# A hybrid layer and two conditioned layers on one core: inputs of rotation issued on SyncE, part of the preparations moved beside the first projection, modulations' sums by rounded products

## The chip, the core and the metric

One core of a Trainium2 chip runs the kernel. The time is the device time of one execution in microseconds (us). The engines are TensorE (PE; PEld is its loading of the stationary operand), VectorE (DVE), ScalarE (ACT), GpSimd (POOL) and SyncE (SP). An "ACTq" or "SPq" row is an instruction of an engine's queue that issues a transfer.

## What is computed

512 tokens of width 1024, all float32. First one hybrid layer:

```python
proj = rmsnorm(x) @ w_in                       # 8 chunks of columns, then the merge gates
ys = (gated_deltanet(...), spatial_gating(u, v, z, ...), rwkv7_time_mix(...), native_sparse_attention(...))
mixed = sum(sigmoid(merge_i) * (ys[i] @ w_branch[i]))
x = rmsnorm(x + mixed @ w_out)
```

Spatial gating is `u * (tril(w_s) @ layernorm(v) + b_s) * silu(z)` in chunks of 128 tokens and four groups of 64 columns. The sparse attention needs a small MLP over blocks of 32 keys (compression) and three tables of distance by slope, masked. Then two layers, each with

```python
mod = silu(c) @ ada_w[l] + ada_b[l]            # 1024 x 6144, one row: shifts, scales, gates
x = x + gate_m * mixer(norm(x) * (1 + scale_m) + shift_m)      # differential and dilated attention, rotated q, k
x = x + gate_f * relu(h @ w_mlp_up)**2 @ w_mlp_down
```

## The kernel before

The kernel is one program of stages. A stage is a block with one list of instructions per engine; between blocks all engines meet (`end_stage` resets the counts that the waits use). Order inside a stage is written out by hand with semaphores (`Signal`); there is no planner. The residual stream `xT` lies in SBUF, features on partitions.

Dense products are made to float32 accuracy from rounded parts: ScalarE copies an operand to float32r (the "hi" part), VectorE subtracts it from the original (the "lo" part), and TensorE adds three rounded products hi x hi, hi x lo, lo x hi in a bank. In the projections (`first_projection` L925, `queries_keys`, `values`) a weight chunk of up to 512 columns is split in four pieces ahead of its use, one piece per tile; in `split_products` (L2304: merge, gates, output) and `mlp` (L3033) the splitting goes on piece by piece, four pieces (two tiles in the MLP) ahead of TensorE. Weights come through a ring of three slots of 2 MB that SyncE fills (`Weights.feed` L251); it waits in its queue for the release of a slot.

The stages that matter here, in order:

- `first_projection`: 33 tiles (t = 0 to 32) in 8 banks; TensorE needs a bank emptied 8 tiles earlier. Tiles 16 to 19 are u and v of gating (gelu on ScalarE), 20 to 23 two gates (silu), 24 to 27 "ab", 28 to 32 keys. ScalarE and VectorE each go through the tiles in order: split a piece of the next chunk, convolve or shift a row, empty a bank. At the end SyncE moves two halves of the keys, once tile 28 is emptied.
- `preparations` (L1282): its inputs are issued at its start, nine on SyncE (L1557 to L1565), six on ScalarE's queue (L1364 to L1368). TensorE: transposes w_s (L1429), transposes the positions (L1432), gate products of RWKV (L1423, L1424), the hidden layer of the compression (L1440, 64 products on halves of the array), gating's products (L1449), compressed keys and values (L1455, L1457), eight transpositions of y (L1462). VectorE has one list: blocks (L1479), decay sums, mean and variance of gating (L1487 to L1497), tables (L1502 to L1506), gate additions (L1512), copy of w_s (L1521), normalisation (L1523 to L1527), g, y (L1540, L1552, L1553), and POOL masks the tables.
- `sparse_attention` with `attention`, then `operands` (L1658), whose end is transpositions into features; the last are those of the sparse attention's y (L1788), copied by ScalarE (L1850). `recurrences` follow.
- `merge` (L2483): 96 pieces, beside which a guest, `Modulation(self, 0)` (L425), forms the first layer's modulations; the MLP of layer 0 holds `Modulation(self, 1)`. The guest loads 1 MB halves of ada_w (issued on ScalarE), VectorE multiplies and adds eight rows of 512 columns (one operation per piece, two per tile in the MLP), and TensorE sums each of the twelve results over partitions (`turn`, L466): four float32 products with one column of ones.
- the output product (`add_products`) with `Turns` (L511) beside it: 13 small inputs (positions, gains) issued by ScalarE ahead of all its work (`beside.load(act)`), tables of sine and cosine on VectorE from its fifth piece on. `RowTail` squares and copies each finished row. `values` of layer 0 has `Reach` beside it, with four inputs, issued the same way.

Of the kernel before, what the change touches and what calls it, by code (L numbers as in the profile page):

```python
# [424 lines left out]
class Modulation:  # L425


    HALVES = 24
    OPS = 4

    def __init__(self, kernel, l):
        self.kernel, self.l = kernel, l
        self.w, self.acc = kernel.take(2, 4, 512), kernel.take(2, 512)
        self.source = kernel.a["ada_w_2"][l]
        self.loads = self.ops = self.turns = 0
# [10 lines left out]
    def multiply(self, dve):  # L446
# [6 lines left out]
        if n % 8 == 0:  # L453
            if c >= 2:
                dve.wait_ge(*k.mod_turned.at(c - 1))
# [10 lines left out]
    def turn(self, pe):  # L466
        k, c = self.kernel, self.turns
        pe.wait_ge(*k.ada_used.at(2 * c + 2))
        for j in range(4):
            ins = pe.matmul(k.bank[7][:, 4 * c + j:4 * c + j + 1], self.acc[:, c % 2, j * P:(j + 1) * P], k.ones[:, 0:1],  # L470
                            start=True, stop=True)
        ins.then_inc(*k.mod_turned.one())
        self.turns += 1

    def finish(self, dve):
        k, l = self.kernel, self.l
        assert self.ops == 4 * self.HALVES
        dve.wait_ge(*k.mod_turned.at(self.HALVES // 2))
        b = PAR["ada_b_2"] + 48 * l
        mod = k.mods[:, l, :]  # L480
        dve.tensor_tensor(mod, k.bank[7][:, 0:48], k.par[:, b:b + 48], ALU.add).then_inc(*k.mod_row.one())
# [7 lines left out]
class RowTail:  # L489
# [7 lines left out]
    def scalar(self, act, k):  # L497
# [3 lines left out]
        if self.by_class is not None:  # L501
# [9 lines left out]
class Turns:  # L511
# [3 lines left out]
    def __init__(self, kernel):  # L515
        R = E // 4 // 2
        self.kernel = kernel
        self.cos, self.sin = kernel.take(NT, R), kernel.take(NT, R)
        self.gains = [kernel.take(2, 2, E) for _ in range(2)]
        self.pos, self.ang, self.n = kernel.take(NT), kernel.take(NT, R), kernel.take(NT, R)  # L520
        kernel.turns = kernel.take(2, 2, 2, NT * 4 * R)
        kernel.row_gain = kernel.take(2, 2, 2)
# [182 lines left out]
class Kernel:  # L705
    def __init__(self, nc, arrays, out):
# [13 lines left out]
        self.arena = sb("arena", [P, ARENA])  # L720

# [25 lines left out]
        self.stored = Signal(nc, "stored")  # L747
        self.moved = Signal(nc, "near_values_moved")
# [22 lines left out]
        self.mod_turned = Signal(nc, "mod_turned")  # L771
# [153 lines left out]
    def first_projection(self):  # L925
        nc = self.nc
# [17 lines left out]
        self.nsa_cmpT = self.take(T)  # L944
        acc = self.take(2, T)
        assert self.top <= ARENA - 2 * SLOT
        self.top -= 2 * T
# [28 lines left out]
        with nc.Block() as block:  # L976
# [28 lines left out]
            def _(act):  # L1005
                for k in range(ND):
                    norm.first_part(act, h[0][:, k, :], k).then_inc(*h_first.one())
                for t, (name, kind, i, lo, n) in enumerate(tiles):
                    if self.w.next_hi < self.w.pieces_until(("p1", name), place[t] + 1):
                        self.w.split_hi(act)  # L1010
                    if t - 2 in convolved:
# [3 lines left out]
                           .then_inc(*self.mixed_act.step(("silu", c)))  # L1015
                    if kind == "features":
                        continue
# [21 lines left out]
            def _(dve):  # L1039
# [21 lines left out]
                def shift(c):  # L1061
# [7 lines left out]
                       .then_inc(*self.mixed_dve.step(("shift", c)))  # L1069
                for t, (name, kind, i, lo, n) in enumerate(tiles):  # L1070
                    if self.w.next_lo < self.w.pieces_until(("p1", name), place[t] + 1):
# [18 lines left out]
            def _(pool):  # L1090
                pool.memset(qkvT[:, :, 0:3], 0.0).then_inc(*self.pool_order.one())
                pool.memset(rwT[:, :, 0:1], 0.0).then_inc(*self.pool_order.one())

            @block.sync
            def _(sp):
                self.w.feed(sp)
                keys = [t for t, tile in enumerate(tiles) if tile[:2] == ("keys", "features")][0]
# [184 lines left out]
    def preparations(self):  # L1282


        nc, a = self.nc, self.a
# [4 lines left out]
        self.y_nsa = self.ysT[:, 0:2, :].rearrange("p k t -> p (k t)").rearrange("p (i c) -> p i c", i=NT)  # L1290
# [20 lines left out]
        self.kcT = self.take(NC)  # L1311
        self.vc = self.take(E)
        self.sel = self.take(H, T)
        self.win = self.take(H, 3 * P)
        self.cmp = self.take(NT, H, NC)
        self.seen = self.take(NT, NC)
        self.gsum = self.take(H)
        keep = self.top
        sel, win, cmp, seen = self.sel, self.win, self.cmp, self.seen
        SLOPES = [2.0 ** (-8.0 * (h + 1) / H) for h in range(H)]  # L1320
        dist = self.scratch[:]
# [5 lines left out]
        def in_h(n, *dims):  # L1327
# [4 lines left out]
        w1, w2, pos_rows, posT = in_h(32, E), in_h(2, E), in_h(2, E), in_h(2, 32)  # L1332
        blocks, hidden = in_h(32, NC), in_h(2, NC)

        gain, bias = self.take(MIX), self.take(MIX)
        w_rows, wT = self.take(H, P), self.take(H, P)
        y, sq = self.take(NT, MIX), self.take(NT, MIX)
        mean, rstd = self.take(NT, H), self.take(NT, H)
        groups = lambda x: x.rearrange("p i (g c) -> p i g c", g=H)
        over = lambda x: x.unsqueeze(3).broadcast_to([P, NT, H, E])  # L1340
        u, v, z = (self.sg[:, :, j * MIX:(j + 1) * MIX] for j in range(3))

        dtb, alog = self.take(H), self.take(H)
        low, small = self.take(NT, H), self.take(NT, H)
        w0a0, up = self.take(2 * MIX), self.take(MIX)
        rwT = self.rwT

        landed = [self.params_landed, self.x_landed, self.moved]
        compress, gating, mixers = landed
        mm, act_done, dve_done, pool_done = self.mm_done, self.act_ready, self.dve_ready, self.pool_ready  # L1350
        mm.order_of(["wT", "pos", ("wa", 0), "hidden0", "hidden1", ("wa", 1), "mixed0", "mixed1", "kc", "vc",
                     ("y", 0), ("y", 1)])
        act_done.order_of(["tanh", "softplus", "alog", "root", "hidden0", "hidden1", ("wa", 0), ("wa", 1), "beta", "cond",
                           ("y", 0), ("y", 1)])
# [1891 lines left out]
```

## Time and profile before

| | us |
|---|---|
| runs: median of 3 (lowest, highest) | 2890.76 (2886.28, 2893.64) |
| the profiled execution | 2882.78 |
| its span, first to last instruction | 2881.0 |
| TensorE busy | 2600.3 (90%) |
| VectorE busy | 1601.1 (56%) |
| ScalarE busy | 1047.2 (36%) |

The time of the profiled execution is its span and a little around it. Busy time is the union of an engine's instructions. A row of a timeline gives the start in us from the span's start, the duration in us (of a merged group: from its first start to its last end), engine, line, operation, output<-inputs, shape and count; in brackets the idle time of the engine before it and what ended it. A matmul of float32 operands that are not rounded stands as two instructions.

### The profile page before, as it was taken

To read this page: it belongs to the slowest core of one execution; us is meant where nothing else is said; L and a number is where in the kernel's file an instruction comes from. 1 tells how busy PE (TensorE), PEld (TensorE's weight loads), DVE (VectorE), ACT (ScalarE), POOL (GpSimd) and SP (SyncE) were. 2 spreads that over 40 slices of the span, in tenths; PEclk is the share of its full clock that TensorE was granted. 3 is DMA by queue.
4 is the path that set the end of the run, shared out by engine and by line. 5 is a ranking of instruction groups with operands and counts; after the bars stand their busy time and mean duration, and the time that the engine had idled before them with its cause. 6 is when DMAs were issued, how large, how long until landed. Compare 5 with 4: busy or idle time off the path is not lost. (4 is left out here: it accounts for less than half of the span.)

```text
span 2881.0 us, 37978 instructions
## 1 busy us (share of the span) xinstructions
PE 2600.3 (90%) x15005; PEld 2078.3 (72%) x15005; DVE 1601.1 (56%) x3039; ACT 1047.2 (36%) x2148; POOL 22.1 (1%) x68
## 2 busy tenths in 40 slices
PE   6986688799889897889989999899979999899999
PEld 5875577688668656767768888687557777688887
DVE  5616756766566586353366765553865333454444
ACT  3225432333355364352332222353644432322221
POOL 0002000000000000000000000000000000000000
PEclk8996888899989998999999999999989999899999
DMA  4220020466412200203335553221002223222220
GB/s 147 78 55 5 10 58 3 132 206 191 152 59 88 93 1 15 84 25 95 112 129 178 184 181 117 88 84 63 30 1 71 53 72 106 88 88 88 102 103 30
DMA packets 212218, 249.56 MB, mean 87 GB/s; under 512 B 13295, under 2 KB 125898, under 8 KB 212042
## 3 DMA queue, kind: packets, MB, share of 16 engines
q1 hardware_dynamic: 178608, 194.22, 20.9%
q10 hardware_dynamic: 33434, 52.91, 5.6%
q8 instruction: 120, 1.97, 0.3%
q14 instruction: 56, 0.46, 0.1%
HBM read 243.70 MB, written 2.10 MB: 85 GB/s over the span
## 5 line engine op out<-in xcount | busy, mean ns | idle before, releaser
L2378 ACT ACTIVATE weights_hi<-weight_ring 128x512 fp32r<-128x512 f32 (+1 forms) x240 | 143.9, 602 | 427.3 <-PE bank L2432 392.6
L2400 DVE TENSOR_TENSOR weights_lo<-weight_ring,weights_hi 128x512 fp32r<-128x512 f32 (+1 forms) x240 | 156.2, 654 | 230.7 <-ACT weights_hi L2378 230.5
L3061 ACT ACTIVATE weights_hi<-weight_ring 128x1024 fp32r<-128x1024 f32 x128 | 135.2, 1057 | 262.9 <-PE bank L3157 261.6
L2432 PE MATMUL bank<-h_hi,weights_hi 128*128 128x512 f32 x512 | 209.8, 410 | 15.8 <-DVE h_lo L2400 8.9
L3157 PE MATMUL bank<-h_hi,weights_hi 128*128 128x512 f32 x512 | 204.4, 399 | 13.0 <-DVE h_lo L422 12.2
L2585 PE MATMUL bank<-chunk_hi,h_hi 128*128 128x512 f32 x448 | 185.2, 413 | 21.2 <-DVE h_lo L422 17.4
L2432 PE MATMUL bank<-h_lo,weights_hi 128*128 128x512 f32 x512 | 204.0, 398 | 0.0
L3157 PE MATMUL bank<-h_lo,weights_hi 128*128 128x512 f32 x512 | 203.6, 398 | 0.0
L2432 PE MATMUL bank<-h_hi,weights_lo 128*128 128x512 f32 x512 | 202.0, 395 | 0.0
L3157 PE MATMUL bank<-h_hi,weights_lo 128*128 128x512 f32 x512 | 201.8, 394 | 0.0
L3157 PE MATMUL bank<-hidden_hi,weights_hi 128*128 128x512 f32 x512 | 199.8, 390 | 0.0
L3157 PE MATMUL bank<-hidden_hi,weights_lo 128*128 128x512 f32 x512 | 199.3, 389 | 0.0
L3157 PE MATMUL bank<-hidden_lo,weights_hi 128*128 128x512 f32 x512 | 199.2, 389 | 0.0
L2585 PE MATMUL bank<-weight_ring_lo,h_hi 128*128 128x512 f32 x448 | 178.9, 399 | 0.0
L2585 PE MATMUL bank<-chunk_hi,h_lo 128*128 128x512 f32 x448 | 177.6, 396 | 0.0
L2432 PE MATMUL bank<-hidden_hi,weights_hi 128*128 128x512 f32 x384 | 152.7, 398 | 20.5 <-DVE hidden_lo L2400 20.5
L3099 DVE TENSOR_TENSOR weights_lo<-weight_ring,weights_hi 128x1024 fp32r<-128x1024 f32 x128 | 156.4, 1222 | 20.5 <-ACT weights_hi L3061 20.4
L460 DVE SCALAR_TENSOR_TENSOR arena<-arena,cond 128x512 f32<-128x512 f32 x168 | 126.1, 751 | 60.0 <-PE bank L2432 57.9
L2432 PE MATMUL bank<-hidden_lo,weights_hi 128*128 128x512 f32 x384 | 151.7, 395 | 0.0
L2432 PE MATMUL bank<-hidden_hi,weights_lo 128*128 128x512 f32 x384 | 151.5, 395 | 0.0
L1197 PE MATMUL bank<-arena 128*128 128x128 f32 (+1 forms) x984 | 135.4, 282 | 6.6 <-ACT arena L1268 6.4
L3129 DVE SCALAR_TENSOR_TENSOR xT<-bank,modulations,xT 128x512 f32<-128x512 f32 x64 | 48.0, 751 | 162.6 <-PE bank L3157 162.6
(487 smaller groups left out, 5377.8 us busy)
## 6 DMA issues: line engine op xcount, KB each, us to landing
arena<-in_ada_w ACTq DMA_DIRECT2D x48, 1024.0 KB, 5.3
weight_ring<-in_w_in SPq DMA_DIRECT2D x21, 2048.0 KB, 7.6
weight_ring<-in_w_in SPq DMA_DIRECT2D x65, 512.0 KB, 5.3
weight_ring<-in_w_mlp_up SPq DMA_DIRECT2D x16, 2048.0 KB, 8.9
weight_ring<-in_w_mlp_down SPq DMA_DIRECT2D x16, 2048.0 KB, 8.0
weight_ring<-in_w_out SPq DMA_DIRECT2D x6, 2048.0 KB, 7.9
weight_ring<-in_w_in SPq DMA_DIRECT2D x10, 1024.0 KB, 7.6
weight_ring<-in_w_branch_a SPq DMA_DIRECT2D x16, 512.0 KB, 6.4
```

The costliest lines, as they stand in the source:

```text
L460: ins = dve.scalar_tensor_tensor(acc, self.w[:, half, j, :], by, acc, ALU.mult, ALU.add)
L1197: ins = pe.matmul(self.bank[O_BANK + g % 2][:, lo:hi], turned[0:k, n % 2, b * P:(b + 1) * P], v, start=b == 0, stop=b == len(u["values"]) - 1)
L2378: act.activation(hi, src, ACT.Copy).then_inc(*hi_done.one())
L2400: dve.tensor_tensor(lo, src, hi.bitcast(F32), ALU.subtract).then_inc(*lo_done.one())
L2432: ins = pe.matmul(out, ws[a_][:, n % PIECES, k - k0, :], tile["x"][b_][:, k, :], start=k + a_ + b_ == 0, stop=last[n] and k == k1 - 1 and ...
L2585: ins = pe.matmul(self.bank[n % 3][:, 0:width], h[a_][:, k, i * P:(i + 1) * P], w[b_][:, k, :], start=k + a_ + b_ == 0, stop=k == ND - 1 a ...
L3061: act.activation(ws[0][:, t % 2], src[t // 4][:, :, c % 4 * P:c % 4 * P + P], ACT.Copy)\
L3099: dve.tensor_tensor(ws[1][:, t % 2], src[t // 4][:, :, c % 4 * P:c % 4 * P + P], ws[0][:, t % 2].bitcast(F32), ALU.subtract).then_inc(*lo_ ...
L3129: dve.scalar_tensor_tensor(self.xT[:, c, :], self.bank[t % NB][:], gate(c), self.xT[:, c, :], ALU.mult, ALU.add).then_inc(*out.one())
L3157: ins = pe.matmul(self.bank[t % NB][:], ws[a_][:, t % 2, k, :], x[b_][:, k, :], start=k + a_ + b_ == 0, stop=k == ND - 1 and a_ == 1)
```

## The change

1. `Turns` and `Reach` issue their inputs on SyncE, ahead of the weights of that stage. `Turns`' lasting tables come first in memory.
2. All inputs of `preparations` are issued by SyncE in `first_projection`, into two ring slots that are free by then. Gating's normalisation and the sparse attention's tables run on VectorE between tiles 22 and 29, their masks on POOL; tanh, cond and the root of the variance on ScalarE.
3. In `preparations`, blocks are formed on 128 partitions; both pairs of gate products have banks of their own and stand first; the transpositions of gating's y move to the end of `operands`.
4. `Modulation`: the accumulated row is split in hi and lo, and two rounded products with a 128x128 of ones give the column sums in all partitions; VectorE takes the diagonals. Nine operations per eight pieces in the merge.
5. `RowTail` squares before it copies.

```diff
 class Modulation:
-    def turn(self, pe):
-        k, c = self.kernel, self.turns
-        pe.wait_ge(*k.ada_used.at(2 * c + 2))
-        for j in range(4):
-            ins = pe.matmul(k.bank[7][:, 4 * c + j:4 * c + j + 1], self.acc[:, c % 2, j * P:(j + 1) * P], k.ones[:, 0:1],
-                            start=True, stop=True)
...
+    def scalar(self, act, n):
+        while 2 <= self.loads < self.HALVES and self.half_done(self.loads - 2) <= n - 2:
+            self.load(act)
+        c = self.due(n, 0)
+        if c is not None:
+            act.wait_ge(*k.ada_used.at(2 * c + 2))
+            if c:
+                act.wait_ge(*k.mod_summed.at(c))
+            act.activation(self.hi, self.acc[:, c % 2, :], ACT.Copy).then_inc(*k.mod_first.one())
+    def tensor(self, pe, n):
+        c = self.due(n, 2)
+        if c is not None:
+            pe.wait_ge(*k.mod_second.at(c + 1))
...
+            pe.matmul(k.bank[7], self.ones, self.hi, start=True, stop=False)
+            pe.matmul(k.bank[7], self.ones, self.lo[c % 2], start=False, stop=True)\
+              .then_inc(*k.mod_summed.one())
+    def vector(self, dve, n):
+        for _ in range(self.steps(n)):
+            if self.ops < self.HALVES * self.OPS:
+                self.multiply(dve)
+        c = self.due(n, 1)
+        if c is not None:
+            dve.wait_ge(*k.mod_first.at(c + 1))
+            dve.tensor_tensor(self.lo[c % 2], acc, self.hi.bitcast(F32), ALU.subtract).then_inc(*k.mod_second.one())
+        c = self.due(n, 3)
+        if c is not None:
+            dve.wait_ge(*k.mod_summed.at(c + 1))
+            dve.tensor_tensor(own, k.bank[7].rearrange("p (j q) -> p j q", j=4),
+                              k.ident[:].unsqueeze(1).broadcast_to([P, 4, P]), ALU.mult).then_inc(*k.mod_row.one())
+            dve.wait_ge(*k.mod_row.all())
+            dve.tensor_reduce(k.mods[:, self.l, 4 * c:4 * c + 4], own, AX_X, ALU.add).then_inc(*k.mod_kept.one())
...
 class RowTail, scalar:
-            act.activation(row, src, ACT.Copy).then_inc(*kernel.act_order.one())
-            row = src
-        self.squares.square(act, k, row)
+            self.squares.square(act, k, src)
+            act.activation(row, src, ACT.Copy).then_inc(*kernel.turned_over.one())
...
 first_projection, scalar:
+                    if (name, i) == ("zz", 1):
+                        act.activation(rwT[0:E, 6, 1:], rwT[0:E, 6, 1:], ACT.Tanh).then_inc(*layer_act.step("tanh"))
+                        act.activation(self.cond, self.par[:, PAR["c_2"]:PAR["c_2"] + ND], ACT.Silu)\
+                           .then_inc(*self.act_order.one())
+                    if (name, i, kind) == ("ab", 1, "tokens"):
+                        act.preload_act_table_set(LN_AND_EXP)
+                        act.wait_ge(*layer_dve.after("var"))
+                        act.activation(rstd, rstd, ACT.Ln).then_inc(*self.act_order.one())
...
 first_projection, vector:
+                steps_at = {22: 1, 23: 2, 24: 1, 26: 1, 27: 2, 29: 1}
                 for t, (name, kind, i, lo, n) in enumerate(tiles):
+                    for _ in range(steps_at.get(t, 0)):
+                        next(normal)
...
 first_projection, sync:
                 self.w.feed(sp)
+                signal, value_ = self.w.released[5]
+                sp.wait_ge(signal.sem, value_)
+                sp.dma_start(self.sg_gain, a["sg_ln_gain"].broadcast_to([P, MIX])).then_inc(*self.sg_landed.dma())
...
+                signal, value_ = self.w.released[6]
+                sp.wait_ge(signal.sem, value_)
+                sp.dma_start(self.gdn_dtb, a["gdn_dt_bias"].broadcast_to([P, H])).then_inc(*landed.dma())
...
 operands, tensor:
-                pe.wait_ge(*act_done.after(("F", "A")))
+                for name, before, y, b0 in (("nsa", "A", self.y_nsa, 4), ("gating", "R", self.y_sg, 6)):
+                    pe.wait_ge(*act_done.after(("F", before)))
...
 merge:
-        guest = Modulation(self, 0)
+        guest = Modulation(self, 0, lambda n: 2 if n % 8 == 7 else 1, (2, 3, 5, 7))
 mlp:
-        guest = Modulation(self, 1) if l == 0 else None
+        guest = Modulation(self, 1, lambda t: 2, (1, 2, 3, 4)) if l == 0 else None
 split_products, and values alike:
             def _(act):
-                if beside is not None:
-                    beside.load(act)
...
             def _(sp):
+                if beside is not None:
+                    beside.load(sp)
                 self.w.feed(sp)
```

The four numbers after `steps` are lags, in pieces or tiles, behind the last multiplication of a sum: hi on ScalarE, lo on VectorE, the products on TensorE, the diagonals on VectorE. TensorE's list in `preparations` is now: positions, gate products 0 and 1 (banks 7, 6 and 5, 4), transposition of w_s, hidden layer, gating's products, compressed keys and values.

## Rows read from the trace of the kernel before

**Rows 1.** The page, part 2: granted clock in 40 slices, tenths of full speed

```profile
PEclk8996888899989998999999999999989999899999
```

**Rows 2.** Windows by stage: stretch, length, busy us (count) by engine, clock, DMA share, GB/s

```profile
203.10:252.20 49.10, 18.84 (x171) 14.65 (x171) 23.75 (x47) 17.93 (x28) 7.07 (x7) 0.55 0.20 42
...
526.00:763.00 237.00, 233.56 (x1056) 192.16 (x1056) 164.42 (x265) 73.97 (x137) 0.00 (x0) 0.99 0.62 190
...
1488.00:1851.00 363.00, 361.90 (x1623) 296.70 (x1621) 226.45 (x296) 87.67 (x104) 0.00 (x0) 1.00 0.45 157
```

**Rows 3.** Timeline of the preparations, first half

```profile
205.75 0.38 SPq L1557 DMA_DIRECT2D arena<-in_sg_w_s  x1
...
212.75 1.12 PE L1429 MATMUL bank<-ident,arena 128*128 128x128 f32 x4 [9.71 <-POOL arena L1402]
213.15 4.90 ACTq L1368 DMA_DIRECT2D hT<-in_nsa_cmp_w  x1
...
220.29 0.37 PE L1432 MATMUL bank<-ident,hT 64*128 64x64 f32 x1 [6.42 <-DMA hT<-in_nsa_cmp_w]
...
220.95 3.79 DVE L1479 TENSOR_TENSOR hT<-arena,hT 64x496 f32<-64x496 f32 x4
...
221.84 0.63 PE L1424 MATMUL bank<-arena 64*128 64x256 f32 x1
...
224.79 7.04 PE L1440 MATMUL bank<-hT 64*64 64x31 f32 x128 [2.33 <-DVE hT L1479]
```

**Rows 4.** Timeline of the preparations, second half, and the next stage's first product

```profile
233.60 1.28 DVE L1512 TENSOR_TENSOR weight_ring<-bank,arena 128x512 f32<-128x512 f32 x2
...
243.28 3.75 PE L1449 MATMUL bank<-arena 128*128 128x256 f32 x8 [6.26 <-DVE arena L1528]
...
248.69 0.67 DVE L1553 TENSOR_TENSOR arena<-arena 128x512 f32<-128x512 f32 x1
...
252.32 1.06 PE L1152 MATMUL bank<-arena 64*128 64x31 f32 x8 [0.94 <-PEq L1360]
```

**Rows 5.** Timeline of the first projection's last tiles, ScalarE and VectorE

```profile
168.42 0.39 ACT L1026 ACTIVATE arena<-bank 128x256 f32<-128x256 f32 x1 [4.19 <-PE bank L998]
...
176.00 0.39 ACT L1029 ACTIVATE arena<-bank 128x256 f32<-128x256 f32 x1 [2.35 <-DVE arena L1084]
...
177.28 1.12 DVE L225 TENSOR_TENSOR weight_ring_lo<-weight_ring,first_chunk_hi 128x920 fp32r<-128x920 f32 x1 [1.37 <-ACT first_chunk_hi L219]
...
203.79 1.28 ACT L1035 ACT_TABLE_LOAD   x1
```

**Rows 6.** Windows inside the preparations, the columns as in rows 2

```profile
203.10:208.20 5.10, 0.00 (x0) 0.00 (x0) 0.20 (x1) 2.07 (x6) 0.84 (x2) 1.00 0.19 57
...
224.80:231.80 7.00, 7.00 (x128) 6.90 (x128) 6.79 (x14) 5.76 (x8) 0.00 (x0) 0.50 0.01 2
```

**Rows 7.** Timeline of the end of the operands' stage, ScalarE

```profile
365.06 1.04 ACT L1850 ACTIVATE arena<-bank 128x1024 f32<-128x1024 f32 x1
```

**Rows 8.** Timeline of TensorE around the first of the merge's sums

```profile
553.88 0.39 PE L2432 MATMUL bank<-h_hi,weights_lo 128*128 128x512 f32 x1
554.11 0.95 PE L470 MATMUL bank<-ones,arena 128*128 128x1 f32 x8
...
555.24 0.39 PE L2432 MATMUL bank<-h_lo,weights_hi 128*128 128x512 f32 x1
```

**Rows 9.** Timeline of the output stage's opening, and TensorE's in layer 0

```profile
763.53 0.39 ACTq L528 DMA_DIRECT2D positions<-in_positions  x1
...
772.89 0.63 ACT L2378 ACTIVATE weights_hi<-weight_ring 128x512 fp32r<-128x512 f32 x1 [12.22 <-issue]
...
774.99 0.76 PE L2432 MATMUL bank<-hidden_hi,weights_hi 128*128 128x512 f32 x1 [12.81 <-DVE hidden_lo L2400]
...
781.39 0.16 DVE L559 CAST arena<-positions 128x4 f32<-128x4 int32 x1
...
1428.21 0.76 PE L2432 MATMUL bank<-hidden_hi,weights_hi 128*128 128x512 f32 x1 [3.85 <-DVE hidden_lo L2400]
```

More of the change, by code:

```diff
@@ L429, with __init__, due @@
     OPS = 4
-    def __init__(self, kernel, l):
+    def __init__(self, kernel, l, steps, lags):
         self.kernel, self.l = kernel, l
-        self.w, self.acc = kernel.take(2, 4, 512), kernel.take(2, 512)
-        self.source = kernel.a["ada_w_2"][l]
-        self.loads = self.ops = self.turns = 0
+        kernel.take(-kernel.top % 8)
+        self.w = kernel.take(2, 4, 512)
+        rounded = kernel.nc.alloc_sbuf_tensor_at(f"modulation_parts_{l}", [P, 1536 + P], F32R,
+                                                 offset=kernel.arena_at + 4 * kernel.top)
+        self.acc = kernel.take(2, 512)
+        self.lo = [rounded[:, 512 * b:512 * b + 512] for b in range(2)]
+        self.hi, self.ones = rounded[:, 1024:1536], rounded[:, 1536:1536 + P]
+        kernel.take(512 + P)
+        self.source = kernel.a["ada_w_2"][l]
+        self.loads = self.ops = 0
+        self.steps, self.lags = steps, lags
+        ops, self.last = 0, []
+        for n in itertools.count():
+            ops += steps(n)
+            while len(self.last) < self.HALVES // 2 and ops >= 8 * len(self.last) + 8:
+                self.last.append(n)
+            if len(self.last) == self.HALVES // 2:
+                break
+        self.end = self.last[-1] + max(lags) + 1
+    def due(self, n, what):
+        n -= self.lags[what]
+        return self.last.index(n) if n in self.last else None
     def load(self, eng):
@@ L517, in __init__ @@
         self.kernel = kernel
+        kernel.turns = kernel.take(2, 2, 2, NT * 4 * R)
+        kernel.row_gain = kernel.take(2, 2, 2)
+        self.end = kernel.top
         self.cos, self.sin = kernel.take(NT, R), kernel.take(NT, R)
@@ L1848, in _ @@
                     features(name, b0)
[L1849 to L1851 removed]
+                for name, row, b0 in (("nsa", 6, 4), ("gating", 2, 6)):
+                    act.wait_ge(*pe_done.after(name))
+                    act.activation(self.ysT[:, row:row + 2, :].rearrange("p c t -> p (c t)"), two(b0), ACT.Copy)\
+                       .then_inc(*act_done.step(name))
             @block.vector
@@ L2411, in _ @@
                 if guest:
+                    for n in range(len(pieces), guest.end):
+                        guest.vector(dve, n)
                     guest.finish(dve)
@@ L2440, in _ @@
                         self.w.release(pe_done)
-                while guest and guest.turns < guest.HALVES // 2:
-                    guest.turn(pe)
+                for n in range(len(pieces), guest.end if guest else 0):
+                    guest.tensor(pe, n)
             @block.sync
             def _(sp):
+                if beside is not None:
+                    beside.load(sp)
                 self.w.feed(sp)
```

388 lines of the change are left out of this document (206 added, 182 removed).

## The prediction

> **What bounds the kernel now.** I read the page first. TensorE's granted clock is full in most slices; the exceptions are the first slices, the fourth (216 to 288 us) and those where one stage hands over to the next [rows 1]. So time comes back in two ways only: TensorE gets less to stream where it is always busy, or a stretch in which it waits gets shorter. Next I read the windows by stage [rows 2]. In the preparations (203.1 to 252.2 us) TensorE is busy 18.84 us of 49.1, at a mean clock of 0.55. In the merge (526 to 763) it is busy 233.56 of 237, in the first layer's MLP (1488 to 1851) 361.90 of 363. There VectorE has 72.6 and 136.6 us free. Last I read the timeline of the preparations in order [rows 3, 4]: the stage opens at 205.75 and waits for its own transfers (the transposition of w_s starts at 212.75, the one of the positions, which everything hangs on, at 220.29). Then VectorE works down one list: blocks, gating's mean and variance, twelve table products, gates, normalisation, and only at 243.28 can TensorE form gating's products.
>
> **Preparations, the largest term.** The thirteen remaining transfers, the normalisation and the tables move into the first projection. I lay the shortened stage out from the same opening, 205.75. TensorE: transposition of the positions 0.37 us, to 206.2. Both pairs of gate products, now in four banks, at 1.2 GHz would take 2.1 us each (220.39 to 222.47 for one pair [rows 3]), the four transpositions 1.12. That makes 211.5. VectorE: two small copies, then blocks as two instructions on 128 partitions in place of four on 64, 2 x 0.95 = 1.9 us, to 208.6; the small sums to 209.0; both gate additions 2 x 1.28 [rows 4], to 211.75; wT 0.7 with its start, to 212.5. The hidden layer's 128 instructions need blocks and their turn behind the transpositions: 7.04 us, 211.5 to 218.55. From the first gating product to the last y product the old stage needs 243.28 to 249.36 = 6.08 us [rows 4], with kc and vc inside it. That gives 224.65, and with the old 0.3 us of hand-over the sparse attention starts at 224.95 in place of 252.32. The transpositions of y and two copies that ended the old stage are gone from it. **Gain 27.4 us** with everything at 1.2 GHz. ScalarE is no bound: with three table loads of 1.28 us [rows 5] its gelu stands ready at 214.6, before the hidden sums.
>
> The clock adds to it. Before, it is still at 2.4 GHz from 203.1 to 208.2, where TensorE does nothing [rows 6]. After, gate products stand in that stretch: 2.5 us of it do the work of 5, so the hidden layer starts at 208.9, 2.6 us sooner. I take **30.0 us**. The ends: 27.4, if the clock falls at once, and 35, if gates, hidden layer and gating's products all run at 2.4 GHz (about half of 7.04 + 3.75 + 5.3 us, less where VectorE's wT at 212.4 is awaited).
>
> The hidden layer's own stretch speaks against the upper end: from 224.8 to 231.8 TensorE is occupied for 7.00 of 7.00 us and the clock stays at 1.2 GHz [rows 6]. The Trainium skill (TensorE: Matmul & The Clock Gate, "What's actually happening") says that activity releases the throttle, which is set by how busy the engine has been. By that rule, with TensorE hardly idle from 205.8 on, the term would be the 35 us end; this row agrees with it only if narrow products count for less.
>
> **What the first projection takes on.** SyncE issues 15 transfers more, in the order gating, compression, gates, from the end of tile 23, at 168.4 us [rows 5]. Before, the six for compression took ScalarE's queue from the stage's opening to 213.15 + 4.90 = 218.05 [rows 3], 12.3 us, and the nine others, on SyncE, some 6; one queue is through at about 187. Behind them stand the two moves of the keys, which wait for tile 28 anyway: four tiles of 3.6 us and one of 5.5 after tile 23, 188.4. They stay in time. Normalisation and tables cost VectorE nine 1.2 us operations and twelve of 0.33, one or two per tile of 3.65 us or 5.5 us, where it now idles 1.37 us before a split, ahead of the wait for the next tile [rows 5]; at tile 27 the 2.5 us put the split 0.3 us late, while the piece is needed 4 us later. ScalarE gets a tanh, cond, two roots and four table loads; it idles 2.35 us or more per tile [rows 5]. TensorE has eight banks of lead. **I take 0**; if the cover goes, the price is the 2 to 3 us of one late piece. POOL's four selections (5.5 us) start after tile 29, at 192.5, and end before 203.
>
> **Operands.** The transposition of y and its copy of 1024 columns join the end, behind nsa's: ScalarE ends the stage, so its 1.04 us [rows 7] adds: **-1.0**.
>
> **Modulations, twice twelve sums.** Before, each sum is eight passes; from 553.88 to 555.24 stand one product, the sum and one product, where products follow each other every 0.23 us [rows 8]: 1.36 - 0.46 = 0.90 us. After, it is two rounded products of 512 columns, 0.46 us. In the merge one of the twelve stood behind the last product and cost nothing: 11 x 0.90 - 12 x 0.46 = 4.4 us; in the MLP 12 x 0.44 = 5.2. **Gain 9.6 us.** VectorE gets three passes of 128x512 more per sum (0.67 us each, as y's product in [rows 4]), 12 x 2.0 = 24 us per stage against 72.6 and 136.6 us free; ScalarE 0.6 us per sum. What is new is a wait: VectorE at lag 7 waits for TensorE's sum at lag 5, one piece later than it would run. Behind it in its queue stand the two passes, then the split of that piece, 2.0 us; TensorE still has two pieces (4.2 us at least) before it. So cost 0; above zero only where this margin fails, and never below.
>
> **Inputs of rotation and reach on SyncE.** Before, ScalarE issues 13 transfers from 763.53 and can split only at 772.89; TensorE idles 12.81 us [rows 9]. The same hand-over in layer 0, without these inputs, idles 3.85 us at 1428.21. 8.96 us saved; but there the clock falls meanwhile and 1428.21 to 1474.5 is 0.9 us longer than 774.99 to 820.4. **Gain 8.1 us.** VectorE meets the inputs at its fifth piece, 781.39 before, 772.1 after; issued at the same absolute times, they land by some 777 to 778. It waits 5 us, while TensorE has pieces until 781.5. The weights issued behind them on SyncE are for 40 us later. In the values stage (945 us) TensorE has split pieces in hand and does not wait for ScalarE: 0. Squares ahead of the copy in the last row: one copy less before the end, **0.6 us**.
>
> **Sum** 30.0 - 1.0 + 9.6 + 8.1 + 0.6 = 47.3 us. The profiled execution took 2882.78 us (span 2881.0); 2835.5. It lies 8.0 us under the median of the three runs, 2890.76; against that median I forecast **2843.5 us**.
>
> **Rivals.**
> (a) The clock stays at 2.4 GHz through the preparations and into the sparse attention, whose first 14 us now run at 1.2: 5 us from the stage, up to 3 from the next: 2835.5. For it: no idle stretch of TensorE over 3 us is left. Against: the hidden layer's 31-column products did not raise the clock in 7 us of full occupancy. 0.18.
> (b) The new chain of each sum eats what the shorter products give: 0 in place of 9.6: 2853. For it: VectorE at 69% in the merge goes to 81%. Against: two pieces of margin. 0.10.
> (c) SyncE's single queue is slow (the compression weights hold it for twice the time), the keys' moves end after 203 and hold the whole stage: 8 us back: 2851.5. 0.06.
> (d) The preparations keep a second wait, on one order of TensorE's list (hidden behind wT, wT behind POOL), and give only half: 2858.5. 0.04.
> (e) Slower: in merge and MLP the pass from accumulator over ScalarE, VectorE and TensorE back lies on TensorE's path, 2.0 + 0.6 = 2.6 us x 24 = 62.4 us. 47.3 - 62.4 = -15.1: 2905.9. It decides once a sum costs TensorE over 1.97 us more (47.3 / 24). Against it: 72.6 us free. 0.03.
> The forecast itself keeps 0.59.
>
> **Numbers.** The range goes from 2831 (case a with 4 us of spread between runs) to 2861 (case d or the low ends of preparations and output stage together, with the spread); outside lie case (e) and the rest of the tails, some 1 in 8. 0.3% (8.7 us) is about what a measurement tells from no change; all cases but (e) lie beyond it. Faster 0.95, same 0.02, slower 0.03.
>
> **What would show it.** Preparations: from the last product of the first projection to the first score some 22 us in place of 49.3; TensorE busy throughout the projection; first wait of VectorE for blocks at once. The granted clock between 208 and 225 decides between forecast and (a). Merge and MLP: no idle TensorE, two products per sum, stages 4.4 and 5.2 us shorter. Output stage: gap near 4 us, VectorE waiting once for a transfer. Wrong if TensorE shows idle time behind the new sums, if the projection's end moves later, or if the sparse attention grows by what the preparations lose.

## The result, and the profile after

The changed kernel takes 2843.6 us (median of 4 runs, 2840.35 to 2848.55) against 2891.32 us; the ratio is 0.9839, interval 0.9819 to 0.9858. 2843.5 had been forecast. The profiled execution took 2843.78 us, its span is 2842.1. So the two traces lie 38.9 us apart and the medians 47.7, while the forecast had 47.3 for the traces. A total that fits this well can hide terms that don't; they are gone through one by one below.

The page, part 2, of the changed kernel: the granted clock in 40 slices, which answers to [rows 1].

```profile
PEclk8998898999989989999999999899989999899999
```

The fourth slice went from 6 to 8. The low spots behind it have moved but not gone. The windows by stage (stretch, length, busy us and count by engine, clock, DMA share, GB/s) answer to [rows 2]:

```profile
32.40:202.80 170.40, 170.16 (x792) 142.81 (x792) 88.91 (x128) 47.42 (x67) 5.90 (x5) 0.99 0.24 70
...
202.80:216.80 14.00, 9.04 (x166) 7.67 (x165) 9.62 (x24) 8.89 (x18) 0.71 (x2) 1.00 0.01 3
499.20:727.10 227.90, 227.75 (x984) 186.49 (x984) 179.29 (x296) 78.56 (x145) 0.00 (x0) 0.99 0.64 195
1452.00:1812.00 360.00, 357.42 (x1548) 289.82 (x1548) 248.08 (x333) 93.66 (x117) 0.00 (x0) 1.00 0.45 158
```

The first projection ends at 202.8 and TensorE is busy in it throughout: what was moved there costs nothing. What was 49.3 us from its last product to the first score is 14.0. The timeline of TensorE in the preparations:

```profile
205.58 0.24 PE L1575 MATMUL bank<-ident,weight_ring 64*128 64x64 f32 x1 [2.76 <-PEq L1086]
...
207.53 0.66 PE L1588 MATMUL bank<-ident,weight_ring 128*128 128x128 f32 x4
208.27 3.92 PE L1593 MATMUL bank<-hT,weight_ring 64*64 64x31 f32 x128
212.12 2.01 PE L1600 MATMUL bank<-arena,hT 128*128 128x256 f32 x8
...
216.78 0.64 PE L1360 MATMUL bank<-arena 64*128 64x31 f32 x8 [2.09 <-PEq L1545]
```

The hidden layer's 128 instructions take 3.92 us where they took 7.04 [rows 3]: the clock is at 2.4 GHz in the whole stage (1.00 in the window above) and falls only at 218.4, in the sparse attention.

The output stage opens like this (TensorE, SyncE's queue and VectorE), beside [rows 9], whose gap begins behind the merge's last sum:

```profile
761.24 0.95 PE L470 MATMUL bank<-ones,arena 128*128 128x1 f32 x8
```

and now:

```profile
731.25 0.77 PE L2535 MATMUL bank<-hidden_hi,weights_hi 128*128 128x512 f32 x1 [4.25 <-DVE hidden_lo L2501]
...
729.12 0.34 SPq L597 DMA_DIRECT2D positions<-in_positions  x1
...
735.86 1.47 SPq L604 DMA_DIRECT2D arena<-in_qk_gain_b  x2
737.37 0.59 SPq L271 DMA_DIRECT2D weight_ring<-in_w_in  x1
...
741.88 0.17 DVE L628 CAST arena<-positions 128x4 f32<-128x4 int32 x1 [3.71 <-DMA arena<-in_qk_gain_b]
```

TensorE's gap is 4.25 us in place of 12.81. The two begin at different places: in the kernel before, the last sum stands 0.8 us into the idle stretch, which from the last product's end (761.40) to the first of the output stage (774.99) is 13.59 us. VectorE waits once, 3.71 us, for the inputs, and TensorE does not idle behind it.

The sums of the MLP are another matter. TensorE, by groups, in the MLP's stretch (name, shapes, count, busy us, mean ns, idle before and its releaser):

```profile
L519 PE MATMUL bank<-modulation_parts 128*128 128x512 f32 x12 | 5.2, 433 | 1.3 <-DVE modulation_parts L532 1.3
```

and around the first of these sums, VectorE and TensorE:

```profile
1482.87 1.53 DVE L483 SCALAR_TENSOR_TENSOR arena<-arena,cond 128x512 f32<-128x512 f32 x2
1484.32 0.68 DVE L532 TENSOR_TENSOR modulation_parts<-arena,modulation_parts 128x512 fp32r<-128x512 f32 x1
...
1485.06 0.49 PE L519 MATMUL bank<-modulation_parts 128*128 128x512 f32 x1 [0.24 <-DVE modulation_parts L532]
1485.39 0.39 PE L520 MATMUL bank<-modulation_parts 128*128 128x512 f32 x1
1485.62 0.40 PE L3260 MATMUL bank<-h_hi,weights_hi 128*128 128x512 f32 x1
```

VectorE forms the low part behind two multiplications, and TensorE stands 0.24 us for it. Such a stop, of 0.24 or 0.30 us, stands at five of the twelve sums; with the first product behind it slower as well (0.33 us to the next start, not 0.23), each of these five sums costs TensorE 0.97 to 1.03 us and not 0.46.

### The profile page after: what moved, and what is told of

It is laid out like the page before. It is cut to its first block and busy times, and to the rows that moved or that the text cites. A ratio compares the mean times of both kernels' runs of the same rounds, so it can differ in the third digit from the quotient of the medians.

```text
span 2842.1 us, 37837 instructions
## 1 busy us (share of the span) xinstructions
PE 2594.4 (91%) x14861; PEld 2069.9 (73%) x14861; DVE 1637.7 (58%) x3110; ACT 1055.5 (37%) x2170; POOL 22.0 (1%) x68
## 5 line engine op out<-in xcount | busy, mean ns | idle before, releaser
L3260 PE MATMUL bank<-h_hi,weights_hi 128*128 128x512 f32 x512 | 203.5, 397 | 13.9 <-DVE h_lo L422 13.2
L1405 PEld LDWEIGHTS bank<-arena 128*128 128x128 f32 (+1 forms) x984 | 123.8, 197 | 16.3 <-ACT arena L1476 14.6
L3186 ACT ACTIVATE arena<-bank 128x512 f32<-128x512 f32 x64 | 38.3, 598 | 256.0 <-PE bank L3260 256.0
```

Of the source, the lines that this page charges most:

```text
L1405: ins = pe.matmul(self.bank[O_BANK + g % 2][:, lo:hi], turned[0:k, n % 2, b * P:(b + 1) * P], v, start=b == 0, stop=b == len(u["values"]) - 1)
L3186: act.activation(relu[:, c % 2, :], self.bank[t % NB][:], ACT.Relu).then_inc(*relu_done.one())
L3260: ins = pe.matmul(self.bank[t % NB][:], ws[a_][:, t % 2, k, :], x[b_][:, k, :], start=k + a_ + b_ == 0, stop=k == ND - 1 and a_ == 1)
```

## The experiments

**The kernel before, once more.** No edit. The layers behind the output stage have the same program in both kernels, apart from the MLP of layer 0, and yet came out longer in the changed kernel's trace: its lead was 43.3 us at the first product of layer 0's projection (834.2 before) and 38.9 at the end, with 2.9 us won in the MLP between.

> The kernel before, unchanged, profiled a second time. The two traces differ by 38.9 us of span, the medians by 47.7 us; stages whose program is the same (layer 0's projections, attention and gates, layer 1) lost 8 to 9 us in the changed kernel's trace, at a lower granted clock. Theory A: that is the chance of a single execution, the first profile of before was a lucky one: here the same program comes out with other lengths in those stages (differences of 1 to 2 us a stage, at another share of time at 1.2 GHz), and the profiled execution is nearer to 2890 than to 2882.8. Rival B: these stages are the same to 0.3 us, and the changed kernel does lose there.

Measured: ratio 1.0004 (0.9993 to 1.0014), profiled span 2891.2 us, 10 us longer than the first profile's. The projection of layer 0's second mixer, in the windows of the kernel before, then of its repetition, then of the changed kernel:

```profile
1107.50:1187.40 79.90, 73.51 (x336) 59.08 (x337) 41.64 (x104) 40.21 (x109) 0.00 (x0) 0.98 0.11 40
```
```profile
1110.10:1192.60 82.50, 76.56 (x337) 61.38 (x337) 41.60 (x104) 40.19 (x109) 0.00 (x0) 0.93 0.12 39
```
```profile
1065.80:1147.90 82.10, 76.17 (x337) 61.57 (x337) 41.60 (x104) 40.20 (x110) 0.00 (x0) 0.94 0.11 39
```

The same program takes 79.9 us at a mean clock of 0.98 and 82.5 at 0.93, and the changed kernel stands with the second. Theory A holds: the first profile was a lucky one. Where a stage is compared below, it is compared over several traces. (That the sparse attention took 68.6 us in the first trace was the same luck: 72.2 in this one, 71.7 and 72.9 in two more with the old preparations, 72.0 in the changed kernel's.)

**Only the inputs on SyncE**, in the kernel before:

```diff
-                if beside is not None:
-                    beside.load(act)
...
+                if beside is not None:
+                    beside.load(sp)
                 self.w.feed(sp)
```

> Before, with only the inputs of rotation and reach issued on SyncE. Forecast 8.1 us: TensorE's gap ahead of the output stage 12.8 to about 4, the output stage 0.5 to 0.9 longer by the clock, values unchanged. Median near 2883. Rival: the transfers come late for VectorE's fifth piece, 3 to 5 us are left.

2881.79 us, ratio 0.9975 (0.9964 to 0.9986): 7.2 us (4.0 to 10.4). TensorE at the hand-over, in its trace:

```profile
762.64 0.95 PE L470 MATMUL bank<-ones,arena 128*128 128x1 f32 x8
767.06 0.76 PE L2431 MATMUL bank<-hidden_hi,weights_hi 128*128 128x512 f32 x1 [3.47 <-DVE hidden_lo L2399]
```

The gap behind the last sum is 3.47 us where it was 12.81 and, in the repetition, 12.39: 8.9 to 9.3 us less. No other stage differs beyond the clock. The forecast of 8.1 stands.

**Only the sums**, in the kernel before (the diff of `Modulation` and its calls, lags as in the change):

> Before, with only the modulations' sums changed. Forecast 9.6 us (4.4 in the merge, 5.2 in the MLP). The changed kernel's trace shows 4.4 in the merge, but in the MLP 5 of the 12 sums stop TensorE for 0.5 us (it waits 0.24 to 0.30 us for the low part), so 2.6 to 3 there: theory 7 to 7.5, median near 2884. Rival: the other work per piece also gets quicker (the merge's products are 0.23 us apart to the third digit differently), then 9 or more.

2878.81 us, ratio 0.9969 (0.9957 to 0.9981): 9.0 us (5.5 to 12.4), too wide to tell 7 from 9.6. The trace tells: the MLP's stage is 367.7 us, 3.0 less than the 370.7 of both traces of before, and not the 5.2 forecast. The merge, from its first product's start to its last one's, is 226.7 us in place of 232.4: 5.7 less, where the sums alone were to give 4.4. So the rival holds for the merge by some 1 us (below), the theory for the MLP, and together they are 8.7 us.

**Only the preparations** (with first projection and operands), in the kernel before, twice:

> Before, with only the first projection, the preparations and the operands changed. Forecast 30.0 - 1.0 = 29.0 us; by the changed kernel's trace the stage itself gives 35.3 us, of which the sparse attention and the operands return 5.1 by a lower clock and the longer end: 30.2. Median near 2861. Rival: 35 us stay, the loss behind it was chance: 2856.

> The preparations' part alone, a second time. Its first trace had the clock down from 205.1, the stage's products at 1.2 GHz and the sparse attention from 223.9; four traces of kernels with the whole change have the same waits and 2.4 GHz throughout (203.9 to 205.6, 11.2 us). Theory: which of the two comes is chance, so the sparse attention starts at 216.8 or 223.9, and single times spread over more than 10 us around 2861. Rival: something in this kernel keeps the stage at 1.2 GHz: 223.9 again, 16 to 17 us at that clock.

2860.85 us, ratio 0.9908 (0.9891 to 0.9925), and 2857.66, 0.9893 (0.9875 to 0.9912): 26.6 and 30.9 us. The windows of the stage in the first and the second execution's trace, the first with its hidden layer, which in the changed kernel took 3.92 us:

```profile
205.70:223.90 18.20, 16.27 (x163) 13.58 (x164) 9.38 (x23) 6.73 (x12) 0.63 (x2) 0.55 0.01 2
```
```profile
210.52 7.04 PE L1521 MATMUL bank<-hT,weight_ring 64*64 64x31 f32 x128
```
```profile
205.40:216.60 11.20, 9.00 (x163) 7.62 (x164) 9.40 (x23) 6.75 (x12) 0.65 (x2) 1.00 0.02 4
```

One program, one list of waits (TensorE idles 2.76 us ahead of the stage in both), and the stage takes 18.2 us at a mean clock of 0.55, or 11.2 at 1.00. The theory holds: which one comes is chance of the execution. Single times spread from 2852.2 to 2869.6 in the first measurement, from 2851.1 to 2858.6 in the second.

**The changed kernel, once more.**

> The changed kernel, unchanged, once more. In its first trace the preparations ran at 2.4 GHz throughout (sparse attention from 216.8); in the trace of the preparations alone, with the same waits, the clock fell at 205.1 and the stage was 7 us longer (from 223.9). Theory: chance of the execution, so the same program shows either, and single times spread over 8 to 15 us; the median stays within 2844 +- 4. Rival: the combination with the other parts keeps the clock up: 216.8 again and a narrow spread.

2838.16 us, ratio 0.9827 (0.9806 to 0.9848), sparse attention from 216.6: 2.4 GHz again. The median lies 1.8 us under the lower end that was expected, and both traces of this kernel are as its rival had them; that one program shows either clock is seen in the preparations alone. In all, eight traces here have the shortened stage behind a gap of 2.8 us or less; seven show it at 2.4 GHz (one of them but for half a us), one at 1.2. Five of the eight have the gap of 2.76 us, the one at 1.2 GHz among them; in the other three it is 0.5 or 1.1.

**Products of no use in the gaps.**

```diff
+                for j in range(10):
+                    pe.matmul(self.bank[t % NB][:], h[0][:, j % ND, 0:P], h[0][:, j % ND, :], start=True, stop=True)
...
+                for j in range(3):
+                    pe.matmul(self.bank[3][:, 0:MIX], wT[:, j, :], v[:, :, 0:E], start=True, stop=True)
...
+                                for j in range(2 if name == "nsa" and lag == 2 and n == 2 else 0):
+                                    pe.matmul(self.bank[7][:, 0:2 * P], self.ident[:], self.sel[:, j, 0:2 * P],
+                                              start=True, stop=True)
```

> The changed kernel with products of no use where TensorE idles around the preparations: ten of 512 columns behind the first projection (2.3 us of the 2.8 us gap), three behind the compressed values, two ahead of the sparse attention's first transposition. Nothing waits for them. Theory (the clock falls because of these gaps): the preparations stand at 2.4 GHz in every execution, the spread shrinks, and the sparse attention gives up to 5 us more (24 us of it stood at 1.2 GHz, half of that at most): median 3 to 8 us under the changed kernel. Rival: the clock falls in the sparse attention by its own narrow products and gaps of 0.2 to 1.3 us: the same time, or 0.5 longer.

2839.01 us, ratio 0.983 (0.981 to 0.9849), against 2838.16 of the changed kernel on the same chip: no gain, where 3 to 8 us had been expected. The gaps are filled (the windows of this kernel's first 31 us of sparse attention and, below it, the changed kernel's):

```profile
216.90:248.00 31.10, 28.46 (x140) 20.52 (x141) 16.53 (x104) 17.82 (x73) 12.75 (x46) 0.67 0.01 1
```
```profile
216.80:247.90 31.10, 27.57 (x131) 19.55 (x132) 16.10 (x101) 17.54 (x72) 12.47 (x46) 0.62 0.00 1
```

The clock falls at 221.5 in place of 218.4 and is low for 20.5 us of the stage, not 23.9; but the stage takes 71.4 us, where the changed kernel's two traces have 72.0 and 71.4. The rival is right: the clock falls inside the sparse attention with a gap of only 0.59 us ahead of it (2.09 in the changed kernel). One thing stays open: in this one trace the operands' stage took 44.6 us and not 49.3, at a higher clock. The time of the whole shows nothing of it, and one trace can't tell whether the products did that or chance.

**The transfers back at the stage's start** (the changed kernel, twelve of the fifteen issued by SyncE in `preparations`):

> The changed kernel with the twelve transfers for compression, gates and decay issued by SyncE at the start of the preparations, not beside the first projection (the three of gating stay). Theory: before, TensorE waited until 220.3 for them, 14.5 us behind the stage's opening at 205.75; with everything else moved the whole wait comes back, 12 to 15 us, and the clock falls in it, so the stage runs at 1.2 GHz (7 us more than in the first trace): sparse attention from 236 to 239, median 2855 to 2862. Rival: most of the term was VectorE's list, not the transfers: 5 us or less.

2850.21 us, ratio 0.987 (0.9848 to 0.9892), 12.0 us over the changed kernel on the same chip. The window of the gap, then of the stage:

```profile
203.60:218.10 14.50, 0.00 (x0) 0.00 (x0) 0.22 (x1) 3.35 (x7) 0.65 (x1) 0.59 0.52 105
218.20:231.70 13.50, 11.31 (x165) 9.60 (x165) 9.38 (x23) 5.54 (x11) 0.06 (x1) 0.81 0.01 2
```

The sparse attention starts at 231.7, 15.1 us later than 216.6. 11.8 us of that is the gap, 2.3 the clock in the stage, the rest a first projection that began 0.9 later. The expectation had the whole stage at 1.2 GHz and 236; the clock was back at 223.4, and the median is 5 us under the lowest expected. Between these traces the operands' stage differs by 3.1 us of clock, so 12.0 are left in the time. So of the 33.6 us that this part got shorter (47.5 in the repetition of before, 14.0 now), 11.8 come back with the wait for these transfers, 14.1 with its clock. The rest, VectorE's list that moved away, the two halves of blocks in one, the order of TensorE and the clock, was not taken apart.

**The sums as before**, all else changed:

> The changed kernel with the modulations' sums as before (eight narrow passes of TensorE in place of two rounded products). Theory: 4.4 us back in the merge from the sums and some 1.3 from the products between them, 2.9 in the MLP: 8 to 9 us over the changed kernel's 2838 to 2844, VectorE 48 us less busy. Rival: the longer chain behind each sum cost what it saved: 4 us or less. Nothing else moves: the sparse attention from 216.7, the gap ahead of the output stage 4.3.

2847.54 us, ratio 0.9866 (0.9847 to 0.9885), 7.8 to 11.3 us over the two measurements of the changed kernel (0.9839, 0.9827). VectorE is busy 1597.9 us in place of 1637.7, 40 less (48 expected). In its trace the merge is 232.4 us from first to last product where all seven with the new sums have 226.7 to 227.5, and the MLP's stage is 3 us longer. The rival falls: what the sums bring is near the forecast. From its trace and five others, the merge's product steps were counted, without sums and the stage's opening at 1.2 GHz: 231 ns a step with the old sums (three kernels), 229 with the new (three kernels), over some 950 steps. 1 us of these 2 is the slower first product behind an old sum (0.32 us), which is part of the 0.90 us that a sum costs; 1 us has no cause that was found.

**Lean: four small edits of the changed kernel.**

```diff
 Modulation.vector:
-        for _ in range(self.steps(n)):
-            if self.ops < self.HALVES * self.OPS:
-                self.multiply(dve)
         c = self.due(n, 1)
         if c is not None:
...
             dve.tensor_tensor(self.lo[c % 2], acc, self.hi.bitcast(F32), ALU.subtract).then_inc(*k.mod_second.one())
+        for _ in range(self.steps(n)):
+            if self.ops < self.HALVES * self.OPS:
+                self.multiply(dve)
 first_projection, scalar:
-                        act.activation(self.ns[:, i, TM_NG:TM_NG + 12], self.bank[t % NB][:, E:E + 12], ACT.Sigmoid)\
-                           .then_inc(*self.act_order.one())
 first_projection, vector:
-                        dve.tensor_copy(self.ns[:, i, TM_VW:TM_VW + E], out[:, 0:E]).then_inc(*self.evac_dve.one())
+                        dve.tensor_copy(self.ns[:, i, TM_VW:TM_VW + E + 12], out[:, 0:E + 12]).then_inc(*self.evac_dve.one())
 preparations, scalar:
+                gates_of = self.ns[:, :, TM_NG:TM_NG + 12]
+                act.activation(gates_of, gates_of, ACT.Sigmoid).then_inc(*self.act_order.one())
...
+                act.preload_act_table_set(LN_AND_EXP)
```

> The changed kernel with four small edits: VectorE takes a sum's low part ahead of that tile's multiplications; the sigmoids of the sparse attention's gates, with their table load, move from the end of the first projection into the preparations (VectorE copies the 12 columns along); the exponential's table is loaded at the preparations' end. Theory: TensorE stands nowhere behind a sum (2.6 us of the MLP's 5 stalls of 0.5), the gap behind the first projection is 1.3 us in place of 2.8 (1.5 to 1.7), the sparse attention starts 0.4 sooner: 4.5 us, and up to 4 more if the shorter gap keeps the clock: median 2836 to 2839. Rival: the sums' stalls come from something else than the low part's place in the queue and stay: 2 us.

2832.35 us, ratio 0.9808 (0.9789 to 0.9826), 5.8 us under the changed kernel on the same chip, 4.5 forecast. The MLP's groups, in its own trace:

```profile
L520 PE MATMUL bank<-modulation_parts 128*128 128x512 f32 x12 | 4.7, 392 | 0.0
L519 PE MATMUL bank<-modulation_parts 128*128 128x512 f32 x12 | 4.7, 389 | 0.0
```

No idle time stands ahead of a sum any more, and the stage takes 365.5 us in place of 367.8: the five stops came from the low part's place in VectorE's queue. The gap behind the first projection is 1.1 us, not 2.8. The sparse attention starts at 215.1 and is no shorter for it. These two make 4.0 us; the trace also has the operands' stage at 46.3 us, not 49.3, at a higher clock, and whether that is chance stays open.

**Leaner: gating's last product on GpSimd** beside the sparse attention:

```diff
-                did(tt(y[:, 0:2], y[:, 0:2], z[:, 0:2], ALU.mult), "y0")
-                did(tt(y[:, 2:], y[:, 2:], z[:, 2:], ALU.mult), "y1")
...
 masks:
+        pool.tensor_tensor(y, y, z, ALU.mult).then_inc(*self.pool_order.one())
```

> As lean, and the last two products of gating (y times the gate, VectorE, 0.67 us each, the end of the preparations) move to GpSimd at the head of its masks beside the sparse attention, where it is idle for over 50 us. Theory: TensorE's gap behind the compressed values goes from 2.0 to 1.0 us (the copies of kc and vc then end the stage), the sparse attention starts 1 to 1.3 sooner, median 1 us under lean (2832.4), 2829 to 2833. Rival: GpSimd's product of 1024 columns slows VectorE beside it, and the sparse attention is 1 us or more longer than 71.3: no gain.

2831.36 us, ratio 0.9808 (0.9792 to 0.9825): the same as lean. TensorE's gap is 1.0 us in place of 2.0, but:

```profile
214.50 2.00 POOL L1727 TENSOR_TENSOR arena<-arena 128x1024 f32<-128x1024 f32 x1 [9.63 <-SPq L1343]
```
```profile
215.23 0.18 DVE L1432 CUSTOM_DVE_ANT_0 arena<-bank,arena 128x31 f32<-128x31 f32 x1
...
215.79 0.75 DVE L1694 TENSOR_TENSOR arena<-arena 128x31 f32<-128x31 f32 x1 [0.19 <-ACT arena L1462]
...
216.76 0.18 DVE L1694 TENSOR_TENSOR arena<-arena 128x31 f32<-128x31 f32 x1
```

and the same product in lean, beside a selection of GpSimd on 128 columns:

```profile
216.58 0.30 DVE L1697 TENSOR_TENSOR arena<-arena 128x31 f32<-128x31 f32 x1 [0.19 <-ACT arena L1462]
```

GpSimd's product runs from 214.50 to 216.50. VectorE's 31-column product of two tiles in SBUF that starts inside that time takes 0.75 us and ends at 216.54, just behind it; the next one, outside, takes 0.18. The operations that read a bank keep their 0.18 us beside it. That hold costs 0.2 us: at the next 128-column operation behind it leaner is 0.35 us ahead of lean, where it started 0.57 ahead. The sparse attention as a whole is 71.9 us in place of 71.3, so the rival is right that much of the gain comes back, but only the 0.2 us is shown to come from GpSimd: two traces of the changed kernel differ by 0.6 in this stage. What is left is too small to be seen in the time.

## Why the prediction was right, and where its steps were not

- **Preparations, 30.0 us (27.4 to 35).** The layout by engines was right: at 1.2 GHz the hidden layer was to run from 211.5 to 218.55 and the sparse attention to start at 224.95, or 222.3 with the clock's help; the one execution at that clock has 210.5 to 217.5 and 223.9. (Its "thirteen remaining transfers" are fifteen, as its later paragraph counts them.) But that is the rarer case. The step that failed is the one on the clock: "the hidden layer's own stretch speaks against the upper end". [Rows 6] show that these narrow products did not raise a clock that was low. They say nothing on whether they keep one that is high, and that was the question: behind a gap of 2.76 us, with no long one inside, it stayed high in four traces of five, and behind the shorter gaps of the other three in all of them. The sentence that followed from the Trainium skill (TensorE: Matmul & The Clock Gate, "What's actually happening") had the 35 us end, and the stage agrees with it: 33.6 us from the repeated trace of before, 35.3 from the first. The same section says that the count of slow products at a kernel's start varies from run to run. Here it is a stage in the middle of the kernel that varies, 18.2 and 11.2 us in one program.
- **Rival (a).** By the sign that the prediction named, the granted clock between 208 and 225, the stage went as rival (a) had it, which was given 0.18, and not as the forecast. Its other half, 3 us from the sparse attention, did not come: 71.7 to 72.9 in three of the four traces of before (68.6 in the first), 71.4 to 72.0 after, and filling the gap ahead of it changed nothing in the stage's length.
- **Up to the recurrences** (preparations less operands, forecast 29.0): from the first projection's first product it is 333.9, 338.8, 336.5 and 334.1 us in four traces with the old stage, 335.8 in the mean, and 305.1 to 305.9 in four with the new one at 2.4 GHz. 30.4 us, and 22.9 in the execution at 1.2 GHz. The medians of the part alone give 26.6 and 30.9. So the net term was right to 2 us. In it the stage is 4.2 us better than forecast (34.2 in the mean of the same traces), and the operands, 45.8 us in the mean with the old stage and 49.4 with the new, give 3.6 back where 1.0 was forecast: 2.6 of clock.
- **Operands, -1.0.** ScalarE's last two copies take 1.94 us together, where one took 1.04 [rows 7]: 0.9.
- **What the first projection takes on, 0.** Right, 170.4 us in both. SyncE was through at 183.9 (187 forecast), the keys' moves were issued at 188.9, GpSimd's selections ran from 192.2 to 198.0 (192.5 to 198).
- **Sums, 9.6 us.** The merge's 4.4 is right: eleven sums of 0.90 us became twelve of 0.45. (The merge got 5.6 shorter; the other 1.2 are the quicker products between the sums, which the prediction does not have.) VectorE's added work was put at 48 us and was 40. The MLP's 5.2 was 2.9. The step that failed is "VectorE at lag 7 waits for TensorE's sum at lag 5 ... TensorE still has two pieces": this checks the merge's lags only, and only the wait of VectorE for TensorE. In the MLP the wait that binds is TensorE's for the low part, one tile earlier, behind two multiplications and the work of the tile. It is rival (b) in a small part, 2.6 us of its 9.6; lean gives 2.3 of them back.
- **Inputs on SyncE, 8.1.** The gap is 4.25 us (3.85 forecast). From the last product's end the old one was 13.59, and 13.0 to 13.2 in four other traces, so 8.7 to 9.3 us went, 9.0 in the mean, where 8.96 were forecast. The output stage behind it, to its last product, took 45.3 to 46.7 us in eight traces with the short gap and 45.4 to 46.7 in five with the long one, 46.1 in the mean of both: the 0.9 us forecast for the clock are not there. VectorE's wait for the inputs was 3.7 us (5 forecast) and harmless. The measured part, 7.2 us (4.0 to 10.4), holds the forecast. The Trainium skill (DMA: Bandwidth & Descriptors, "Issuing engines are not separate DMA queues") calls the sequencer's time for an issue usually small against the transfer; here these 13 issues stood 9.4 us ahead of ScalarE's first split, and TensorE with it, so what counts is who waits behind the issuing engine.
- **Last row, 0.6.** The gap behind the output stage went from 4.5 to 4.0: 0.5.
- **The sum.** By parts 7.2 + 9.0 + 28.7 + 0.5 = 45.4 us; the whole gave 46.6 and 50.0 in its two measurements, each to some 5 us; by the stages in the traces it is 30.4 + 5.6 + 2.9 + 9.0 + 0.5 = 48.4. The forecast of 47.3 lies among them. Its misses, 2.3 too much for the MLP's sums, and too little for the preparations' net (1.4), the merge (1.2) and the output stage (0.9), largely cancel. So the net gain was foreseen within the noise, but that 2843.6 stands 0.1 us from 2843.5 is luck; the repetition gave 2838.2. The 38.9 us between the two traces, taken alone, would have read as 8 us too few: that is the first profile's luck. The prediction's remark that this profile lay 8.0 us under the median was the warning.
- **Case (e).** "All cases but (e) lie beyond" 8.7 us is a slip: (e), 15.1 us slower, lies beyond it too. Nothing hangs on it.

## What to carry to other kernels

Check every edge of a new chain at every place where it is used, in both directions: the lag that holds in one stage, with one operation a piece, fails in the next with two a tile, and one reordering of the consumer's queue mends it. Ask of the clock two questions, what raises it and what keeps it: work that can't do the first may do the second, so a stage whose last long wait is removed can come out with its products at twice the speed as well (7.04 and 3.92 us for the hidden layer here). And compare stages that the change doesn't touch before the others; where those differ, the trace differs by chance, and a second profile of the same kernel costs less than a false explanation.

## What was not expected of the hardware

- One program's stage of 11.2 us at 2.4 GHz took 18.2 in another execution, with equal waits; and behind a gap of 14.6 us the clock was back after 5.2 us of the same stage (218.2 to 223.4), while in the execution of 18.2 us it stayed down from 205.1 to 222.1 with TensorE at work from 205.7. Gate products of 256 columns ran at the stage's start in both; what tells the two apart stays open.
- A 31-column product of VectorE took 0.75 us beside a 128x1024 product of GpSimd and ended with it; the same one took 0.30 in lean, beside a 128-column selection, and operations that read a bank were as fast as ever.
- The merge's products follow each other 1 ns faster with the new sums, over 950 products 1 us, for no reason that was found.
